# Two output columns of a weight block: their products in turn instead of one after the other

## What is computed

```
for i in range(DEPTH_2):                     # 4 layers
    mod_l = (silu_c @ w_mod[i] + b_mod[i])   # 6 rows of 1024, for latent and for context tokens
    h_l = rms_norm(x_lat, g_norm_mix[i]) * (1.0 + sc1_l) + sh1_l
    y_c, y_l = mixer(h_c, h_l, ...)          # GLA, convolution, attention, GLA
    x_lat = x_lat + gt1_l * y_l
    h_l = rms_norm(x_lat, g_norm_mlp[i]) * (1.0 + sc2_l) + sh2_l
    x_lat = x_lat + gt2_l * sq_relu_mlp(h_l, w_mlp_in[i], w_mlp_out[i])
    # the same for the context tokens, except in the last layer

def sq_relu_mlp(h, w_in, w_out):
    return jnp.square(jax.nn.relu(h @ w_in)) @ w_out
```

## Time and profile before

| | |
|---|---|
| executions | 3039.8, 3045.49, 3039.91 us |
| median | 3039.91 us |
| profiled execution, first to last instruction (its span) | 3043.6 us |
| granted TensorE clock, mean over the span | 0.982 |
| busy: PE matmul, PE weight load | 95%, 78% |
| busy: DVE, ACT, POOL | 60%, 39%, 10% |
| chain that ended last: PE, DVE, ACT | 84%, 8%, 5% |
| products in `three` (L595, L596, L597) on that chain | 25%, 24%, 24% |

### The profile page before, as it was taken

The page is one execution under the profiler, slowest core; times in us unless marked ns, Lnnn a source line. Parts: engine busy times, 40 slices in busy tenths (PEclk is TensorE's granted clock), DMA queues, the critical chain, the costliest instruction groups (busy, mean ns, idle before and its releaser), DMA issues.

```text
span 3043.6 us, 43496 instructions
## 1 busy us (share of the span) xinstructions
PE 2902.9 (95%) x18494; PEld 2360.8 (78%) x18494; DVE 1837.3 (60%) x2559; ACT 1192.8 (39%) x1674; POOL 304.2 (10%) x282
## 2 busy tenths in 40 slices
PE   8999888998999999999999999998999999998999
PEld 7888888997855788877667887876678887774899
DVE  4477766555456467764875777546647775546554
ACT  3245564445234422234344222344442223425443
POOL 1000002101001211111011100200120011000110
PEclk9999999999999999999999999999999999998999
DMA  8836324454211244432113444320034442221353
GB/s 290 332 132 236 125 84 166 180 181 154 97 42 42 111 166 169 177 138 98 57 53 128 180 173 153 122 110 28 15 139 155 177 180 111 98 70 42 132 187 125
DMA packets 59602, 407.54 MB, mean 134 GB/s; under 512 B 6504, under 2 KB 9832, under 8 KB 11024
## 3 DMA queue, kind: packets, MB, share of 16 engines
q1 hardware_dynamic: 58368, 401.05, 36.0%
q0 software_dynamic: 1040, 3.71, 0.4%
HBM read 403.65 MB, written 1.09 MB: 133 GB/s over the span
## 4 chain that ended last, share of the span: by engine, by line
PE 84%; DVE 8%; ACT 5%; issue 2%; POOL 1%; DMA 0%; DVEq 0%; ACTq 0%
PE bank L595 25%; PE bank L597 24%; PE bank L596 24%; DVE wlo L1960 3%; ACT whi L1330 2%; PE bank L1084 1%; PE bank L1134 1%; ACT part L1587 1%; PE bank L1078 1%; PE bank L1209 1%; PE bank L695 1%; PE bank L1088 1%; PE bank L1225 1%; ACT xnhi L1590 1%; PE bank L719 0%
## 5 line engine op out<-in xcount | busy, mean ns | idle before, releaser
L1960 DVE TENSOR_TENSOR wlo<-raw,whi 128x2048 fp32r<-128x2048 f32 x282 | 649.7, 2304 | 456.9 <-ACT whi L1330 456.8
L1330 ACT CAST whi<-raw 128x2048 fp32r<-128x2048 f32 x282 | 537.3, 1905 | 618.7 <-PE bank L597 613.7
L595 PE MATMUL bank<-xnhi,whi 128*128 128x512 f32 (+1 forms) x1776 | 669.4, 377 | 39.1 <-DVE xnlo L2373 19.1
L597 PE MATMUL bank<-xnhi,wlo 128*128 128x512 f32 (+1 forms) x1776 | 655.3, 369 | 0.0
L596 PE MATMUL bank<-xnlo,whi 128*128 128x512 f32 (+1 forms) x1776 | 654.3, 368 | 0.0
L595 PEld LDWEIGHTS bank<-xnhi,whi 128*128 128x128 f32 x1776 | 338.9, 191 | 137.4 <-issue 59.9
L597 PEld LDWEIGHTS bank<-xnhi,wlo 128*128 128x128 f32 x1776 | 339.0, 191 | 57.8
L596 PEld LDWEIGHTS bank<-xnlo,whi 128*128 128x128 f32 x1776 | 339.3, 191 | 54.0 <-issue 0.2
L595 PE MATMUL bank<-hidhi,whi 128*128 128x512 f32 (+1 forms) x1024 | 373.3, 365 | 0.0
L596 PE MATMUL bank<-hidlo,whi 128*128 128x512 f32 (+1 forms) x1024 | 372.2, 363 | 0.0
L597 PE MATMUL bank<-hidhi,wlo 128*128 128x512 f32 (+1 forms) x1024 | 372.1, 363 | 0.0
(11 more groups left out here) (327 smaller groups left out, 4082.6 us busy)
## 6 DMA issues: line engine op xcount, KB each, us to landing
raw<-in_wall SPq DMA_DIRECT2D x318, 1024.0 KB, 4.8
vraw<-in_wall SPq DMA_DIRECT2D x60, 1024.0 KB, 4.8
x<-in_x SPq DMA_DIRECT2D x2, 1024.0 KB, 6.6
bias<-relative_offsets POOLq DMA_DIRECT2D x2, 768.0 KB, 6.8
x<-relative_offsets POOLq DMA_DIRECT2D x2, 768.0 KB, 9.3
out<-x SPq DMA_DIRECT2D x1, 1024.0 KB, 4.8
vec<-in_vec SPq DMA_DIRECT2D x1, 665.0 KB, 10.2
cst<-in_cst SPq DMA_DIRECT2D x1, 492.0 KB, 11.5
```

The source lines that it names most:

```text
L595: mm(out, wh, xh, start=first, stop=False)
L597: return mm(out, wl, xh, start=False, stop=last)
L1330: nc.scalar.copy(b.whi[u % SPL][:], b.raw[pos % RAW][:]).then_inc(*R.made("hi_ready"))
L1960: ttn(b.wlo[u % SPL][:], b.raw[blocks[u] % RAW][:], b.whi[u % SPL][:], ALU.subtract).then_inc(*R.made("lo_ready"))
```

## The change

A new branch stands ahead of the loop over columns. It is taken by units that are not `tokens_out`, `fresh` or `single` and have no `between`. It waits for both columns' banks at once, then goes through the row blocks; for each it runs the three kinds of product, and each kind for column 0 and column 1, so that the bank changes after every product. Number, operands and sizes of the products stay. Each column's last product still raises `chunk_ready`; column 0's is now the last product but one of the unit.

```diff
         s = g["unit"] % SPL
         pe.wait_ge(*R.next("lo_ready"))
+        if not (tokens_out or fresh or single or between):
+            for c in range(2):
+                if g["chunks"] + c >= 4:
+                    pe.wait_ge(*R.next("chunk_taken"))
+            for k in range(kc):
+                for w_of, x_of in ((b.whi, x[0]), (b.whi, x[1]), (b.wlo, x[0])):
+                    for c in range(2):
+                        last = mm(bank[2 * s + c][:, 0:t], w_of[s][:, k, c * P:(c + 1) * P], x_of[:, k0 + k, 0:t],
+                                  start=(k == 0 and w_of is b.whi and x_of is x[0]),
+                                  stop=(k == kc - 1 and w_of is b.wlo))
+                        if k == kc - 1 and w_of is b.wlo:
+                            last.then_inc(*R.made("chunk_ready"))
+            g["chunks"] += 2
+            g["unit"] += 1
+            return
         for c in range(1 if single else 2):
             both = 2 if single else 1
             if g["chunks"] >= 4:
```

## The result

| | before | after |
|---|---|---|
| median of the runs | 3040.42 us | 3170.77 us (3166.24 to 3183.33) |
| ratio, 95% interval | | 1.0428 (1.0413 to 1.0442) |
| span of the profiled execution | 3043.6 us | 3181.5 us |
| granted TensorE clock in it | 0.982 | 0.968 |

The change costs 130 us by the medians, 138 between the two profiled executions. Direction and places were right, the sizes were not.

What follows compares the result with a forecast made beforehand. TensorE's gapless matmul stream, 95% of the span, was taken as the bound. Terms 41 + 3 + 19 + 17 + 4 + 7 = 91 us, on a median of 3039.91, gave 3131 us; range 3086 to 3168.

Steps and rivals of the forecast that it cites:

- a): From mlp_in to mlp_out, 12 times: TensorE stalls 3.3 us, or 3.8 in part 3, for column 1's late low half; 41 us.
- b): Weight splits queued behind the late copy in mlp_in: 0.5 us late with seven multiplies, nothing with six; 3 us.
- c): TensorE's clock falls behind the twelve mlp_out stalls: 1.6 us each, 19 us in all, ends 0 and 34.
- d): At the norms, the sum waits for column 0's later square and POOL's add: 2.8 us for five norms; 17 us in all.
- clock behind the norms: Clock loss behind the lengthened norm waits: not in the forecast's sum, only in a rival.
- e): Turn of the summed modulations in the last mlp_out: TensorE waits 1.3 us for DVE's copy, three layers; 4 us.
- f): Units with 256 tokens: late weight low halves cost between 0 and 0.4 us a unit, taken as 0.15 for 48; 7 us.
- rate of products: In alternated units on TensorE: the step from product to product stays unchanged; 0 us.
- faster rival: Alternated products run faster because accumulating into one bank holds up the next: at best 119 us gained, 3012; chance 0.06.
- the fall in the stream: Rival: pauses at bank changes lower the clock within the alternated products, 117 us on top, 3248; chance 0.03.
- six multiplies 4.25: DVE's next-layer modulation multiplies in an mlp_in unit, standing ahead of column 1's product: taken to last 4.25 us.
- a rival, at 10 us: The clock falls everywhere, also behind the norms: 34 us for 19, and 1.4 more for seven norms, 3156; chance 0.2.

Runs made afterwards that it cites:

- filled_waits: Changed kernel plus 16 products into an unused bank ahead of the wait for row 7 in each mlp_out's first unit, layers 0 to 2: 3154.52 us, 1.0368.
- norms_filled: Kernel before with products alternating only in the nine units ahead of a norm, plus two 0.9 us filling products ahead of each norm's wait: 3062.80 us, 1.0053.
- tokens_256_only: Kernel before with products alternating only in units with 256 tokens, without those ahead of norms: 3055.46 us, 1.0047.
- where_slack_2: Kernel before with products alternating in 51 MLP units where queues have slack, and DVE's multiplies behind both columns in all mlp_in units: 3043.04 us, 0.9999.
- mlp_in_only: Kernel before with products alternating only in mlp_in of layers 0 to 2, less units behind norms: 3131.96 us, 1.0295.
- norms_only: Kernel before with products alternating only in the nine units ahead of a norm: 3071.94 us, 1.0100.
- short_low_half: Changed kernel, but in parts 1 to 3 of MLPs of layers 0 to 2 POOL makes each unit's first low half for 32 of 512 tokens: 3154.16 us, 1.0364.
- low_halves_together: Changed kernel, but POOL waits for both columns' high parts before making the first low half of an mlp_in unit, layers 0 to 2: 3172.90 us, 1.0424.
- before_filled: Kernel before with filling products into an unused bank in its own longer waits, behind norms and in units 107 and 108: 3054.39 us, 1.0035.

## Why the prediction was right in kind and too small

| term | forecast | measured | from |
|---|---|---|---|
| a) twelve waits | 41 | 49 | 46.1 idle, + 12 x 0.26 |
| b) late weight blocks in mlp_in | 3 | 13 | 3 x (1.18 + 1.14 + 1.96) |
| c) clock behind the twelve waits | 19 | 16 to 21 | filled_waits, medians and profiles |
| d) norms | 17 | 21 | 23.8 - 4.8 idle, + 6 x 0.26 |
| clock behind the norms | 0 | up to 9 | norms_filled |
| e) turn | 4 | 4 | 4.0 idle |
| f) 256 tokens | 7 | 10 to 15 | tokens_256_only |
| rate of products | 0 | 0 | where_slack_2 |
| sum | 91 | 113 to 132 | 130 measured |

The parts measured alone do not add up to the whole. By the medians mlp_in_only 91, norms_only 32, tokens_256_only 15 and the turn 4 make 142 against 130; between the profiled executions 82, 26, 10 and 4 make 122 against 138. So the sum is known to some 15 us only, and whether one part changes what another costs (as by the clock falling at other places when waits move) was not shown.

**The rate: right.** The step over a change of bank in the earlier trace rows carried over to a change after each product: 2448 such products cost nothing. The faster rival is out, and so is the fall in the stream: behind the wait shown above the alternated units of mlp_out run at a clock of 0.99 (same columns as the windows above).

```profile
2594.00:2632.50 38.50, 38.50 (x171) 30.66 (x169) 24.34 (x36) 6.52 (x4) 0.00 (x0) 0.99 0.50 185
```

The Trainium skill, TensorE: Matmul & The Clock Gate, section A second HAM failure mode, cited in the prediction, puts the loss that it reports down to small pauses between groups of products; no run here has them at a change of bank.

**a) and b): the chain right, one duration wrong.** The step that failed is "six multiplies 4.25" (and with it "seven multiplies, 4.72"): six took 5.09 in the unit shown, and seven 5.75 at the end of part 3 of layer 2 (from 2679.20). The 4.25 comes from a row beside which POOL was idle. The change moves ACT's copy of column 0 up to the start of the multiplies, so POOL makes column 0's low half beside them. The working followed column 1's low half, which took 1.26 where 1.28 was forecast, and never asked when column 0's would run. short_low_half takes most of that POOL work away and gives the forecast's numbers: waits of 3.1 to 3.2 in parts 1 and 2 (3.3 forecast), 1.4 us of late blocks in three layers (3 forecast). With the collision b) is 13: the weights behind six multiplies were forecast to be late by 0.02 us, so most of each further delay is paid (in part 2 of layer 2 six multiplies take 5.29 for 4.25, 1.04 longer, and PE then idles 0.86 for the weights). Of the some 39 us that the forecast lacked, a) and b) are 18, and short_low_half, which undoes this one error in three of four parts, is 17 faster than the changed kernel. The rest is the clock behind the norms (up to 9), f) (3 to 8) and d) (4).

In the trace of the changed kernel the third multiply of the unit, which meets POOL, has a row of its own, behind that of the first two:

```profile
2582.23 1.41 DVE L2060 SCALAR_TENSOR_TENSOR modacc<-vraw,cond,modacc 128x512 f32<-128x512 f32 x2
2583.74 1.60 DVE L2060 SCALAR_TENSOR_TENSOR modacc<-vraw,cond,modacc 128x512 f32<-128x512 f32 x1
```

POOL's low half starts at 2583.04, while the second multiply runs (to 2583.64), and is 0.48 longer than alone (1.74 for 1.26); the multiply that starts next, while POOL runs (to 2584.78), is 0.85 longer than usual (1.60 for 0.75). The Trainium skill, SBUF — State Buffer, section Who interferes with whom, states this: a DVE instruction with two inputs in SBUF contends with a GpSimd instruction that reads SBUF, and whoever comes second waits. The rows agree, in both directions. low_halves_together agrees too: the weights' low half has two such inputs, and it is what POOL then delays.

**c): right, at the size forecast.** 1.3 to 1.8 us a wait, where 1.6 was taken.

**d): the waits right, the clock behind them left out of the sum.** The wait at L787 in the unit shown is 2.83, as forecast (2.8). That the clock falls behind such waits stood in a rival, at 10 us; it is up to 9. Before, PE idled 2.46 us behind the sum's products; now it idles 2.8 in front of them as well. With that alone changed (norms_only) the mean granted clock is 0.978 to 0.980, where seven of nine executions of the kernel before on that chip have 0.982 to 0.983.

**e): right.** 4.0 in three waits.

**f): the cost of a late block undersized.** 0.25 a unit in ffn_in where 0.15 was taken, from bounds of 0 and 0.4: the weights are late by 0.26 where the working had 0.12, and the wait costs as much again. The last layer's mlp_out, costed at nothing, loses some 0.2 a part.

**The range** fell short because its upper end took only the clock and f) upwards; a) was given a third downwards and nothing upwards, b) neither, though durations read from rows in which the other engine was idle got longer here, not shorter.

## What to carry to other kernels

Before two results are made to end together, list every engine's queue between them and see what stands in front of the second: that work had the second half of the unit as its cover. A duration taken from a trace holds for the neighbours it had there; when a change moves an instruction, look up what then runs beside it on engines that delay each other, as DVE and POOL do here. The idle stretches of 3.5 to 4.1 us cost 1.3 to 1.8 us more in clock here, and products that fill such a wait gave 16 us of 130 back. They must end before what they wait for (before_filled lost 9 us by outlasting it), and behind the kernel's own waits they gave only some 5.

## What the runs showed that was not expected

- DVE and POOL delay each other where they meet: a multiply of 0.75 us takes 1.60 and a low half of 1.26 takes 1.74. Over the kernel that is 39 us of DVE time (327.0 against 288.3) and 20 of POOL's low halves of the hidden columns.
- A POOL subtraction on 32 columns takes 0.70 us where 512 take 1.27: less than half of its time goes with its size.
- Behind idle stretches of 1.6 to 2.2 us the clock stayed at its full level at seven of nine places; filling a wait halfway was worth as much as filling it whole (3154.57 and 3154.52 us).
